# Index projection of a sparse-attention block: columns three units behind, early weights in places of their own, rows on two engines

## The reference

```python
cond = jax.nn.silu(c)
mod = jnp.einsum('bd,de->be', cond, w_ada[l]) + b_ada[l]
sh1, sc1, g1, sh2, sc2, g2 = [m[:, None, :] for m in jnp.split(mod, 6, axis=-1)]
h = rmsnorm(x, norm1_g[l]) * (1.0 + sc1) + sh1
proj = jnp.einsum('bsd,de->bse', h, w_in[l])
...
x = x + g1 * jnp.einsum('bsm,md->bsd', mix, w_out[l])
```

## Time and profile before

| | us |
|---|---|
| median of 3 runs | 3682.78 (3681.52 to 3685.25) |
| span of the profiled execution | 3673.6 |
| TensorE busy | 3250.9 |
| VectorE busy | 2538.3 |
| ScalarE busy | 1831.4 |
| first product of unit 0 | 59.01 |
| end of unit 35 | 328.45 |

### The profile page before, as it was taken

The page is one execution under the profiler, slowest core; times in us unless marked ns, Lnnn a source line. Parts: engine busy times, 40 slices in busy tenths (PEclk is TensorE's granted clock), DMA queues, the critical chain, the costliest instruction groups (busy, mean ns, idle before and its releaser), DMA issues. The chain is left out here.

```text
span 3673.6 us, 44993 instructions
## 1 busy us (share of the span) xinstructions
PE 3250.9 (88%) x15808; PEld 2610.3 (71%) x15808; DVE 2538.3 (69%) x4800; ACT 1831.4 (50%) x3051; POOL 368.9 (10%) x587
## 2 busy tenths in 40 slices
PE   4986888899797798977789989889989999999999
PEld 3775666777685576755667768768868887888887
DVE  6542688877892677676776657788887875665676
ACT  3211677877673787878867643332232222322233
POOL 1010011110101100000000000012212220000131
PEclk8997999999896899999899999989999999999999
DMA  6354333322336432111111124644454445664565
GB/s 220 126 196 121 106 105 102 95 84 67 103 101 189 127 99 65 48 45 32 39 35 30 52 101 162 218 149 155 147 171 155 155 146 206 223 235 155 199 214 206
DMA packets 334617, 475.95 MB, mean 130 GB/s; under 512 B 29056, under 2 KB 218704, under 8 KB 333984
## 3 DMA queue, kind: packets, MB, share of 16 engines
q1 hardware_dynamic: 285936, 308.29, 26.6%
q0 software_dynamic: 48464, 164.88, 12.7%
HBM read 316.07 MB, written 156.98 MB: 129 GB/s over the span
## 5 line engine op out<-in xcount | busy, mean ns | idle before, releaser
L2099 PE MATMUL m_ps<-m_h,w_hi 128*128 128x512 f32 x1792 | 560.7, 395 | 43.1 <-DVE m_h L1728 21.0
L2099 PEld LDWEIGHTS m_ps<-m_h,w_hi 128*128 128x128 f32 x1792 | 340.9, 191 | 117.7 <-DVE m_h L1728 30.0
L928 DVE SCALAR_TENSOR_TENSOR rank<-spare,iw,rank 128x1024 f32<-128x1024 f32 (+5 forms) x330 | 332.1, 1021 | 69.7 <-ACT spare L857 64.5
L2116 PE MATMUL m_ps<-w_hi,a_hi 128*128 128x512 f32 x896 | 350.7, 391 | 12.0 <-DVE w_lo L1936 8.9
L2099 PE MATMUL m_ps<-m_h,w_lo 128*128 128x512 f32 x896 | 352.7, 394 | 0.0
L2116 PE MATMUL m_ps<-w_lo,a_hi 128*128 128x512 f32 x896 | 350.2, 391 | 0.0
L2116 PE MATMUL m_ps<-w_hi,a_lo 128*128 128x512 f32 x896 | 350.1, 391 | 0.0
L857 ACT ACTIVATE spare<-isps 128x1024 f32<-128x1024 f32 (+5 forms) x352 | 279.7, 812 | 114.5 <-PE isps L825 80.7
L825 PE MATMUL isps<-ki,iq_hi 128*128 128x512 f32 (+3 forms) x608 | 238.8, 394 | 88.9 <-ACT spare L857 68.7
L2659 ACT ACTIVATE pt<-tps 128x512 f32<-128x512 f32 (+1 forms) x432 | 233.3, 573 | 109.6 <-PE tps L2598 53.1
L2598 PE MATMUL tps<-ident,probs 128*128 128x128 f32 x1632 | 238.7, 287 | 46.0 <-DVE probs L2814 28.7
(11 more groups left out here) (285 smaller groups left out, 7032.8 us busy)
## 6 DMA issues: line engine op xcount, KB each, us to landing
w_raw<-in_w_ff SPq DMA_DIRECT2D x136, 512.0 KB, 5.3
dram_aop<-a_out POOLq DMA_DIRECT2D x224, 256.0 KB, 2.6
a_lo<-dram_aop SPq DMA_DIRECT2D x56, 1024.0 KB, 5.3
ada_w<-in_w_ada POOLq DMA_DIRECT2D x16, 1024.0 KB, 6.6
q_hi<-dram_proj_hi SPq DMA_DIRECT2D x128, 128.0 KB, 3.0
q_lo<-dram_proj_lo SPq DMA_DIRECT2D x128, 128.0 KB, 3.0
iq_hi<-dram_proj_hi SPq DMA_DIRECT2D x224, 64.0 KB, 2.4
iq_lo<-dram_proj_lo SPq DMA_DIRECT2D x224, 64.0 KB, 2.5
```

What stands on the lines that cost most here:

```text
L928: nc.vector.scalar_tensor_tensor(out=dst, in0=got, scalar=w, in1=dst, op0=ALU.mult, op1=ALU.add).then_inc(s_acc, 1)
L2099: mm = nc.tensor.matmul(ps[:, b], w[:, m % WOPS, k, :], hop[:, j, h, :, k, :], start=fresh and k == 0 and i == 0, stop=k == KH - 1 and i == 2,
L2116: mm = nc.tensor.matmul(ps[:, t], a[:, c % RING, k, t * P:(t + 1) * P], w[:, c % RING, k, :], start=first and i == 0, stop=last and i == 2 ...
```

## The change

1. **Columns three units behind.** `ADA_FROM = EARLY * NG - 2` is 7 where the first chunk's sums stood behind unit 12: chunks 4 to 11 are now summed behind units 7, 10, ..., 28, and their columns run ahead of units 10, 13, ..., 31. Unit 7 is evacuated in the middle of group 3's rows.
2. **Raw weights.** Tiles 1 and 2 get places in `w_early`, loaded by SP; POOL's loads are put in another order.
3. **Rows.** Odd rows of u are made by ScalarE. `ht_lo` is awaited block by block in every group.
4. **Tokens.** ScalarE scales group 0's tokens. Squares are cut in two halves and interleaved one group ahead; `norms(g + 1)` stands ahead of the evacuation of unit 3g-1. SP's wait ahead of group 1's load is gone. In group 0, `turn(1, 0)` and `turn(1, 1)` stand behind units 1 and 2.

```diff
+    ADA_FROM = EARLY * NG - 2
+            return ada_first[:, 0 if g == 1 else 2, 0:2, :].rearrange("p a b -> p (a b)")   # junk(g), g > 0
+            return u[:].rearrange("p a b -> p (a b)")                                       # junk(0)
+        def raw(i):
+            return w_early[:, i - 1] if i in (1, 2) else w_raw[:]
         def ada_after(n):
-            i = (n - EARLY * NG) // 3
+            i = (n - ADA_FROM) // 3
...
 # POOL
-                load_w(1)
-                load_w(2)
                 load_ada(4)
                 load_w(3)
+                load_ada(5)
                 load_w(4)
-                load_ada(5)
+                load_w(5)
                 load_ada(6)
-                load_w(5)
                 load_ada(7)
                 load_w(6)
                 load_ada(8)
                 load_w(7)
                 load_ada(9)
+                load_w(8)
                 load_ada(10)
-                load_w(8)
                 load_ada(11)
 # SP
-                sp.wait_ge(s_ss, TG)
+                for i in (1, 2):
+                    tile = INDEX_TILES[i]
+                    sp.dma_start(raw(i), w_view[:, :, tile * P:(tile + 1) * P]).then_inc(s_we[i - 1], 16)
                 sp.dma_start(xt(1)[:], x_view[1]).then_inc(s_x[1], 16)
 # ScalarE
+                def first_parts(g, ks):
+                    for k in ks:
+                        n = g * KT + k
+                        if k % 2:
+                            act.wait_ge(s_tp, n + 1)
+                            if n >= 2:
+                                act.wait_ge(s_hh, n - 1)
+                                act.wait_ge(s_hl, n - 1)
+                            nc.scalar.activation(u[:, 1, :], tps[:, k % 4, :], ACT.Identity, bias=keep.cols[:, 1, k:k + 1],
+                                                 scale=keep.cols[:, 0, k:k + 1]).then_inc(s_uo, 1)
+                        act.wait_ge(s_uo if k % 2 else s_ue, n // 2 + 1)
                         nc.scalar.activation(ht_hi[:, g, k, :], u[:, k % 2, :], ACT.Copy).then_inc(s_hh, 1)
...
-                norms(0)
-                for i in range(EARLY):
-                    split_w(i)
-                first_parts(0)
+                squares(0, range(TG))
+                split_w(0)
+                root(0)
+                act.wait_ge(s_rstd, 1)
+                for t in range(TG):
+                    nc.scalar.activation(xt(0)[:, t, :], xt(0)[:, t, :], ACT.Copy, scale=rstd[:, t:t + 1]).then_inc(s_xn, 1)
+                split_w(1)
+                split_w(2)
+                squares(1, range(0, 2))
+                act.wait_ge(s_cols, 1)
+                first_parts(0, range(KT))
+                squares(1, range(2, TG))
+                root(1)
                 for g in range(1, NG):
-                    norms(g)
                     evac(EARLY * (g - 1))
-                    first_parts(g)
+                    first_parts(g, range(0, KH))
+                    if g + 1 < NG:
+                        squares(g + 1, range(0, 2))
+                    evac(EARLY * g - 2)
+                    first_parts(g, range(KH, KT))
+                    if g + 1 < NG:
+                        squares(g + 1, range(2, TG))
+                        root(g + 1)
+                    evac(EARLY * g - 1)
 # VectorE: activations(g)
+                        if k == KH:
+                            if g:
+                                evac(EARLY * g - 2)
+                            else:
+                                split_w(1)
+                        if k < KT and k % 2 == 0:
...
-                for h in range(2):
-                    ada_sums(2, h)
-                norms(0)
-                split_w(0)
+                ada_sums(2, 0)
+                variance(0)
+                ada_sums(2, 1)
+                inverse(0)
                 for h in range(2):
                     ada_sums(3, h)
-                split_w(1)
-                split_w(2)
-                then(norm_cols(0, B_SC1, B_SH1, 4))
-                activations(0)
+                split_w(0)
+                norm_cols(0, B_SC1, B_SH1, 4).then_inc(s_cols, 1)
+                dve.wait_ge(s_cols, 1)
+                activations(0)
+                split_w(2)
+                norms(1)
                 for g in range(1, NG):
-                    norms(g)
                     evac(EARLY * (g - 1))
                     activations(g)
+                    if g + 1 < NG:
+                        norms(g + 1)
+                    evac(EARLY * g - 1)
 # TensorE
-                        if n == 0:
-                            pe.wait_ge(s_hl, k + 1)
+                        if i == 0:
+                            pe.wait_ge(s_hl, KT * g + k + 1)
...
-                    if ada_after(n - 2) is not None:
-                        columns(ada_after(n - 2))
+                    if ada_after(n - 3) is not None:
+                        columns(ada_after(n - 3))
...
-                        if g + 1 < NG and i < 2:
-                            turn(g + 1, i)
+                        part = i - 1 if g == 0 else i
+                        if g + 1 < NG and part in (0, 1):
+                            turn(g + 1, part)
```

More of the change, by code:

```diff
@@ L100, in __init__, with index_projection @@
         self.neg_lam = sb("neg_lam", [P, 1])
-def index_projection(nc, keep, scr, x, w_in, ht_hi, ht_lo, xt_first, ada_first, lamt, c, norm1_g, norm2_g, w_ada, b_ada,
+def index_projection(nc, keep, scr, x, w_in, ht_hi, ht_lo, xt_first, ada_first, lamt, w_early, c, norm1_g, norm2_g, w_ada, b_ada,
                      lam_q1, lam_k1, lam_q2, lam_k2):
@@ L162, in index_projection @@
         s_tp = sem("s_x_transposed")
-        s_u = sem("s_h")
+        s_ue = sem("s_h_even")
+        s_uo = sem("s_h_odd")
         s_hh = sem("s_h_hi")
@@ L166, in index_projection @@
         s_w = sem("s_w_in")
+        s_we = [sem(f"s_w_early_in{n}") for n in range(2)]
         s_whi = sem("s_w_hi")
@@ L204, in junk @@
             if g:
-                return ada_first[:, 2, 0:2, :].rearrange("p a b -> p (a b)")
-            return xt_second[:, 0, :]
+                return ada_first[:, 0 if g == 1 else 2, 0:2, :].rearrange("p a b -> p (a b)")
+            return u[:].rearrange("p a b -> p (a b)")
+        def raw(i):
+            return w_early[:, i - 1] if i in (1, 2) else w_raw[:]
         def ada_after(n):
-            i = (n - EARLY * NG) // 3
-            return len(FIRST_CHUNKS) + i if n >= EARLY * NG and (n - EARLY * NG) % 3 == 0 and i < EC - 4 else None
+            i = (n - ADA_FROM) // 3
+            return len(FIRST_CHUNKS) + i if n >= ADA_FROM and (n - ADA_FROM) % 3 == 0 and i < EC - 4 else None
         with nc.Block(no_gpsimd_drain=True) as block:
@@ L219, in load_w @@
                     if i:
-                        pool.wait_ge(s_wlo, i)
+                        pool.wait_ge(s_wlo, 1 if i == EARLY else i)
                     pool.dma_start(w_raw[:, :, 0:cols], w_view[:, :, tile * P:tile * P + cols]).then_inc(s_w, 16)
@@ L284, in split_w @@
                 def split_w(i):
-                    act.wait_ge(s_w, 16 * (i + 1))
+                    if i in (1, 2):
+                        act.wait_ge(s_we[i - 1], 16)
+                    else:
+                        act.wait_ge(s_w, 16 if i == 0 else 16 * (i - 1))
                     if i >= WS:
                         act.wait_ge(s_mm, through[i - WS])
-                    nc.scalar.activation(w_hi[:, i % WS], w_raw[:], ACT.Copy).then_inc(s_whi, 1)
+                    nc.scalar.activation(w_hi[:, i % WS], raw(i), ACT.Copy).then_inc(s_whi, 1)
                 def evac(n):
@@ L299, in evac, with squares @@
                     e.then_inc(s_ehi, 1)
-                def norms(g):
+                def squares(g, tiles):
                     act.wait_ge(s_x[g % 2], 16 * (g // 2 + 1))
-                    for t in range(TG):
+                    if g == 1:
+                        act.wait_ge(s_acc, 2 * KT)
+                    for t in tiles:
                         if g or t:
@@ L307, in norms, with root @@
                                              accum_out=ss[:, g * TG + t:g * TG + t + 1]).then_inc(s_ss, 1)
+                def root(g):
                     act.wait_ge(s_var, g + 1)
@@ L310, in norms @@
                     nc.scalar.activation(rstd[:, cols], rstd[:, cols], ACT.Sqrt).then_inc(s_std, 1)
[L312 to L316, removed]
+                def first_parts(g, ks):
[9 more added lines that the diff above has]
+                        act.wait_ge(s_uo if k % 2 else s_ue, n // 2 + 1)
                         nc.scalar.activation(ht_hi[:, g, k, :], u[:, k % 2, :], ACT.Copy).then_inc(s_hh, 1)
-                    if g:
-                        evac(EARLY * g - 1)
                 act.wait_ge(s_c, 16)
@@ L324, in _ @@
                 nc.scalar.activation(lams[:, 2:4], lams[:, 0:2], ACT.Exp).then_inc(s_exp, 1)
-                norms(0)
-                for i in range(EARLY):
-                    split_w(i)
```

(38 more changed lines are left out.)

4 lines of the change are left out of this document (removed).

## The result

The changed kernel takes 3648.2 us (3646.9 to 3649.9, 4 runs) where the one before takes 3682.2; the ratio is 0.9904 (0.9890 to 0.9917). A second set of runs gave 3647.3 against 3684.8, 0.9900 (0.9885 to 0.9914). The forecast was 3643.3, so the gain is 34 to 37 us where 39.5 were forecast.

A forecast was written before the change was run, and what follows sets the result against it. TensorE, busy 88% of the span, was taken as the bound, losing time to the start, token waits and columns stops with low clock. Savings of 4.4 + 0.3 + 3.9 + 30.9 = 39.5 us gave 3643.3 us, range 3632 to 3661.

The forecast's parts named there:

- The projection's end, 39.5 us earlier: End of the index projection: 4.4 + 0.3 + 3.9 + 30.9 = 39.5 us sooner, with unit 35 ending at 289.
- Start, 4.4 us: Before unit 0: rows as if begun at 49.1, not 53.50; group 1's tokens land at 47.5 and hold ScalarE's first copy.
- Units 1 to 11: Projection's first token groups: 83.9 us instead of 87.8, 3.9 saved, unit 11 ending at 146.0; bounds 73.4 and 94.4.
- The stops ahead of groups 2 and 3: TensorE waits for normalised tokens: 4.6 us plus 1.7 of low clock before group 2, 2.9 us before group 3.
- the stop in unit 9: Chunk 4's sums on VectorE in the middle of group 3 make unit 9's last low part 1.3 us late.
- Units 12 to 35, 30.9 us: Steady part: 143.0 us instead of 173.9, as waits at columns go, clock stays up, and 1.0 is added for late chunks.
- The sum's last line: Whole kernel: span 3673.6 becomes 3634.1; 9.2 us taken as outside the span are kept, giving 3643.3.
- Low clock at `columns`: Rival, steady part: the clock falls at columns as before, 12.1 us more, 3655; chance 0.17.
- Early loads: Rival: second token group lands by 43, third by 92; 3.8 and 2.9 us less, 3636.5; chance 0.17.
- No change: Rival: the projection ends earlier but the next stage gives the time back, 3683; chance 0.03.
- slower: Rival: late chunk sums on VectorE hold back evacuations, so TensorE lacks product buffers; 3697 at a landing of 18; chance 0.02.
- One sign: Sign that the forecast is right: TensorE's granted clock is 1.00 from group 3 on.

The follow-up runs named there:

- squares_after: The changed kernel, but ScalarE squares all of group 1's tokens behind group 0's rows, not two tiles ahead of them: 3638.1 us, one run.
- load_early: The changed kernel, but SP loads group 3's tokens ahead of its wait for unit 2's evacuation, not behind that unit's store: 3637.9 us, one run.
- cols_only: The kernel before with only the columns part of the change, including the changed order of GpSimd's loads: 3653.9 us, ratio 0.9915 (0.9901 to 0.9928).

## Why the prediction came out as it did

**The projection's end, 39.5 us earlier: right.** The first traces have 38.9, and the second ones 43.0 (331.4 and 288.4).

**Start, 4.4 us: right, and by its reason.** The load of group 1's tokens landed at 47.8 (taken: 47.5), the first copy came at 50.0 (49.9), unit 0 at 61.8 (62.1). What undoing the raw tiles costs (8 us) and what the late squares hold back at unit 0 (5.2 us, `squares_after`) was measured one by one.

**Units 1 to 11: near in the sum, in part by luck.** They take 86.0 and 84.6 us in the two traces where 83.9 was forecast. The stops ahead of groups 2 and 3 are 3.96 and 3.30 us (3.72 in the second trace) where 4.6 and 2.9 were worked out, and the second comes from the load behind unit 2's store, as `load_early` shows. The 2.9 leave out the 0.7 us for variance, root and reciprocal that the bullet before it counts; with them it is 3.6. But the stop in unit 9 did not happen, and could not: `EARLY * NG - 2` is 10, not 7. The description of the change ahead of the prediction has the same slip. The chunks are summed behind units 10, 13, ..., 31 and their columns run ahead of units 13, ..., 34, so that nothing stands in group 3's rows. The sum thus has 1.3 us for a stop that isn't there and 1.0 for a `columns` that comes later. It lacks the low clock behind the stop ahead of group 3 (16 transposes in 3.67 us and unit 7 in 6.92, where 1.91 and 5.85 are the times at full clock: 2.8 us), since it had low clock only once, and 1.5 us in unit 3, whose last blocks wait for rows (7.32 us for it). The two sides cancel in part and leave the 2 us by which the first trace is longer.

**Units 12 to 35, 30.9 us: right.** 141.8 us (289.5 less 147.8) for 143.0: eight `columns` at 0.9 instead of seven at 1.0, and no wait for a late chunk, for which 1.0 was added. That the clock would stay up was taken from the nearest rows; `cols_only` and the changed kernel show it.

**The sum's last line: a wrong term that cancels.** The prediction says that the median of the runs has 9.2 us outside the span. Outside the span are 1.8 us (3645.1 and 3646.9 are one execution). The 9.2 were the distance between the median and a trace whose own execution was, by these 1.8, some 7 us faster. Since the saving is taken from the median in the end, the constant cancels: 3643.3 is 3682.8 less 39.5. But the same outlying trace is why the first pair of spans shows only 28.5 us. The runs show a gain of 34 and 37 us, the projection's end in the traces 38.9 and 43.0. The intervals reach to 40.5 and 42.4: they hold 38.9 and the forecast's 39.5, but not 43.0. Whether the 2 us or more between runs and traces are scatter or a small loss behind the projection is left open.

**The rivals and the signs.** Low clock at `columns`: fell, 1.00. Early loads: fell; group 1's tokens landed at 47.8 and group 3's at 98.9, where 47.5 and 97 were forecast. No change and slower: fell; no chunk held TensorE at all. One sign did not come: the clock was to be 1.00 from group 3 on, and it is 0.50 over the 5 us from 113, behind the stop ahead of that group. No table load stands before an odd row: the projection has two, as before the change.

## What to carry to other kernels

Where an engine waits at regular places for sums that another makes in between, move the reader to the first place that lies behind the end of the sums, and count what the clock gives back too: here a third of the 39 us lay in products that ran at half clock behind the waits. An engine that works in order should have no operation with a late load ahead of one that is on the path; here two squares in front of the first copy and one store in front of a load cost 3.7 and 4.8 us at the projection's end. Check a constant such as `EARLY * NG - 2` against the loop that uses it before you place its waits: here it gave a stop that could not occur. Before a difference between two traces is explained, take a second trace of each: here one of them was 10 us off in a part that no one had edited.

## What was not expected of the hardware

The part behind the projection, the same work in the same order, took 3345.2 to 3356.9 us in twelve traces. It goes with the time at low clock in it (379 to 421 us, worked out from the granted clock in windows of 40 us; correlation 0.72, 0.2 us for each us), so some of the scatter may lie there; what else makes it is open. Filling 1.8 us of standing still in each stop with useless products kept the granted clock at 1.00, 2.4 GHz, through 160 us. Without them it fell behind six of the eight stops and stayed up behind two.
